# FFN-up with 512-column matmuls: rows and their remainders pass one rounded weight together, and ScalarE, VectorE and GpSimd share the rest

## The chip, the cores and the metric

The kernel runs on one core of a Trainium2 chip. The metric is the time of one execution on the device in microseconds (us), the median of several runs. The engines are called PE (TensorE), ACT (ScalarE), DVE (VectorE), POOL (GpSimd) and SP (SyncE, which issues most DMAs). The trace is of one profiled execution; its times are counted from the start of the span.

## The reference

The program computes two transformer blocks for 256 tokens of width 1024: first attention with a mixture of 32 experts, then a second block that ends with a gated feed-forward network (FFN). Only the FFN's first half is touched by the change:

```python
D_FF_2 = 2816
FFN_CONV_W = 3
...
        h = rms_norm(x, g_pre_ffn[l])
        up = causal_dwconv(h @ w_up[l].astype(h.dtype), w_conv_ffn[l], b_conv_ffn[l])
        c_u, c_g = jnp.split(up, 2, axis=-1)
        ffn = (jax.nn.gelu(c_g, approximate=True) * c_u) @ w_down[l].astype(h.dtype)
        x = x + rms_norm(ffn, g_post_ffn[l])
```

`w_up` is 1024 x 5632. The convolution runs over positions, three taps for each of the 5632 channels.

## The kernel before

**Rounded matmuls in three parts.** PE multiplies in a rounded fp32 format. To keep precision each operand is split in a rounded part (hi) and a remainder (lo), and a product is hi·hi + hi·lo + lo·hi. Each loaded megabyte of weights (128 x 2048 values) has a number s in the list `SPL` of splits; 34 to 55 are the 22 loads of `w_up`, 56 to 66 those of `w_down`. ACT rounds (`split`, L768) into one of two buffers of the tensor `W`, in turn, so the rounding of s waits until PE has done s-2. DVE then makes the remainder (`split`, L1237), and PE waits for that with `lo_done(s)`. The rows of h, turned so that the 256 tokens lie along the free dimension, are in `X`: `xin[0]` is X's rounded part, `xin[1]` its remainder, each with eight blocks k of 128 channels.

**FFN-up.** Split 34 + i' holds 256 output channels, taken as two banks of PSUM (m = 0, 1), each 128 channels x 256 tokens. The banks of the stage are `U_cv[0]` to `U_cv[43]`, n = 4i + 2·half + m, where i runs over 11 pairs of splits, half 0 is the branch u and half 1 the branch g. PE computes a bank in `columns_in`, by `mm3` (L1952): for each of eight k three matmuls of 256 columns, with the weight (hi, hi, lo) as stationary operand, so 48 for a split. `columns_first` (L2036) does split 34, part by part.

**After PE.** For each bank ACT makes `tmp` = last tap times bank plus bias (Identity, L1210); DVE adds the other two taps, shifted by one and two tokens, reading the bank in PSUM (L1920 and L1923), and the second of them releases the bank. When both banks of a g half are done, ACT takes GELU of them (L1215) and DVE multiplies the branches into `fT` (L1929). ACT and DVE work strictly in the order in which the program issues. In the loop over i, half, m, with m = 1, the rounding (ACT) and the remainder (DVE) of split 36 + 2i + half stand ahead of that bank's own work.

**The down projection.** For 22 blocks k of f, ACT rounds fT (`inner`, L1194) and DVE makes the remainder (L1904) into `X`, whose blocks come free as PE leaves them. The first six are issued inside the FFN-up loop, ahead of the last bank's work (i = 10, half = 1, m = 1). PE then runs 264 matmuls of 512 columns. Before any of them it waits for the remainder of split 56 and of block 0 of f.

GpSimd's part in the neighbourhood are three products in the recurrent layer before the FFN (L745 to L751) and four products with the gain of a norm (L728); it has nothing to do in the FFN. SP refills a slot of the ring of eight when DVE has made the remainder of the split that lay there.

## Time and profile before

| | us |
|---|---|
| median of 3 runs | 1410.02 (1408.59 to 1410.97) |
| profiled execution, span from first to last instruction | 1408.3 |
| PE busy (6969 matmuls) | 1286.9 (91%) |
| DVE busy | 486.8 (35%) |
| ACT busy | 401.2 (28%) |
| POOL busy | 59.1 (4%) |
| mean granted PE clock | 0.986 of full speed |

The profiled execution has no time of its own beside its span; the median lies 1.7 us above it. About two thirds of the span is the mixture of experts, bound by DMA; the FFN-up stage lies between 1212 and 1342 us, the down projection between 1342 and 1402. A row of the timeline reads: start, duration, engine, line and operation, output<-inputs, partitions x columns, count; in brackets the idle time of that engine before it and who ended that. Instructions on DVE and ACT overlap their neighbour by 0.05 to 0.1 us, so the distance from start to start is a little shorter than a duration. Durations of matmuls contain the way through the array; only their spacing tells what one costs. A row of the windows view gives the stretch, its length, then busy us and instructions of PE, PE's weight loads, DVE, ACT and POOL, then the granted PE clock as a share of full speed, the share of DMA and its GB/s. A row by line and form gives the count, then busy us, mean ns of one, idle before.

### The profile page before, as it was taken

To read this page: it belongs to the slowest core of one execution; us is meant where nothing else is said; L and a number is where in the kernel's file an instruction comes from. 1 tells how busy PE (TensorE), PEld (TensorE's weight loads), DVE (VectorE), ACT (ScalarE), POOL (GpSimd) and SP (SyncE) were. 2 spreads that over 40 slices of the span, in tenths; PEclk is the share of its full clock that TensorE was granted. 3 is DMA by queue.
4 is the path that set the end of the run, shared out by engine and by line. 5 is a ranking of instruction groups with operands and counts; after the bars stand their busy time and mean duration, and the time that the engine had idled before them with its cause. 6 is when DMAs were issued, how large, how long until landed. Compare 5 with 4: busy or idle time off the path is not lost.

```text
span 1408.3 us, 16583 instructions
## 1 busy us (share of the span) xinstructions
PE 1286.9 (91%) x6969; PEld 737.3 (52%) x6969; DVE 486.8 (35%) x730; ACT 401.2 (28%) x643; POOL 59.1 (4%) x115
## 2 busy tenths in 40 slices
PE   8999999999999889998888988889888999899998
PEld 7888433343333333333333332333324898799986
DVE  5895312112111111111211111111114687677765
ACT  5684212100110001100001000010004766655554
POOL 4001000000000000000000000000000510000000
PEclk9999899999999999999999999999999999899999
DMA  9548699999999999999999999999999964355520
GB/s 337 165 148 307 259 393 429 428 427 427 426 428 427 429 428 426 429 426 427 428 427 428 428 428 427 428 427 428 426 429 370 245 213 150 121 184 186 188 100 30
DMA packets 78474, 480.79 MB, mean 341 GB/s; under 512 B 5504, under 2 KB 40475, under 8 KB 53568
## 3 DMA queue, kind: packets, MB, share of 16 engines
q1 hardware_dynamic: 75904, 474.76, 83.3%
q0 software_dynamic: 2496, 4.96, 1.7%
q8 instruction: 57, 0.93, 0.3%
q14 instruction: 17, 0.14, 0.0%
HBM read 478.39 MB, written 1.31 MB: 341 GB/s over the span
## 4 chain that ended last, share of the span: by engine, by line
PE 52%; DMA 38%; DVE 4%; ACT 3%; issue 1%; DVEq 0%; ACTq 0%
DMA arena<-in_w_dn_dram 38%; PE ps L1952 22%; PE ps L2357 11%; PE ps L2397 11%; PE ps L2324 1%; PE ps L2413 1%; DVE W L1237 1%; PE ps L2036 1%; PE ps L1960 1%; PE ps L2514 1%; PE ps L2287 1%; ACT arena L960 0%; ACT arena L910 0%; PE ps L2368 0%; ACT W L768 0%
## 5 line engine op out<-in xcount | busy, mean ns | idle before, releaser
L2357 PE MATMUL ps<-ring,arena 128*64 128x512 f32 x1392 | 316.5, 597 | 12.0 <-DMA ring<-in_w_gu_dram 12.0
L2357 PEld LDWEIGHTS ps<-ring,arena 128*64 128x64 f32 x1392 | 97.4, 137 | 210.1 <-issue 179.1
L1952 PE MATMUL ps<-X,W 128*128 128x256 f32 x1560 | 191.4, 286 | 2.2 <-DVE W L1243 1.9
L1952 PEld LDWEIGHTS ps<-X,W 128*128 128x128 f32 x1560 | 190.2, 194 | 3.3 <-DVE W L1243 2.3
L1588 DVE TENSOR_SCALAR arena<-ps 128x512 f32<-128x512 f32 x32 | 22.1, 692 | 479.1 <-PE ps L2357 479.1
L1952 PE MATMUL ps<-W,X 128*128 128x512 f32 (+2 forms) x780 | 172.8, 380 | 2.7 <-issue 1.6
L1237 DVE TENSOR_TENSOR W<-ring,W 128x2048 fp32r<-128x2048 f32 (+2 forms) x64 | 144.9, 2264 | 78.9 <-ACT W L768 78.9
L2397 PE MATMUL ps<-ring,arena 128*64 128x512 f32 x648 | 145.7, 594 | 21.9 <-DMA ring<-in_w_dn_dram 21.9
L1952 PEld LDWEIGHTS ps<-W,X 128*128 128x128 f32 x780 | 141.5, 188 | 31.0 <-DVE W L1237 3.8
L973 ACT ACTIVATE arena<-arena 128x512 f32<-128x512 f32 x32 | 20.2, 630 | 460.2 <-DVE arena L1588 460.2
L2357 PE MATMUL ps<-arena 128*64 128x512 f32 x656 | 150.5, 599 | 0.0
L768 ACT ACTIVATE W<-ring 128x2048 fp32r<-128x2048 f32 (+2 forms) x65 | 122.6, 1887 | 81.5 <-PE ps L1952 80.5
L2397 PEld LDWEIGHTS ps<-ring,arena 128*64 128x64 f32 x648 | 48.4, 137 | 116.4 <-issue 115.8
L2397 PE MATMUL ps<-arena 128*64 128x512 f32 x376 | 85.8, 598 | 23.9 <-DMA arena<-in_w_dn_dram 23.9
L1616 DVE SCALAR_TENSOR_TENSOR X<-ps,arena,X 128x512 fp32r<-128x512 f32 x32 | 24.0, 751 | 219.7 <-ACT X L986 219.7
L986 ACT ACTIVATE X<-ps,arena 128x512 fp32r<-128x512 f32 x32 | 22.0, 687 | 258.4 <-PE ps L2397 258.4
L2357 PEld LDWEIGHTS ps<-arena 128*64 128x64 f32 x656 | 46.9, 138 | 91.1 <-issue 90.4
L2397 PEld LDWEIGHTS ps<-arena 128*64 128x64 f32 x376 | 25.1, 136 | 84.1 <-DMA arena<-in_w_dn_dram 42.4
L2324 PEld LDWEIGHTS ps<-X,W 128*128 128x128 f32 x256 | 33.7, 197 | 25.5 <-issue 24.9
L716 POOL CAST W<-arena 128x128 fp32r<-128x128 f32 x32 | 9.3, 293 | 871.0 <-PE ps L2357 851.4
L2413 PE MATMUL ps<-X,W 64*128 64x512 f32 x256 | 39.4, 425 | 6.5 <-DVE X L1616 6.5
L2368 PE MATMUL ps<-ident,arena 128*128 128x128 f32 x128 | 21.5, 291 | 25.6 <-ACT arena L960 25.6
(350 smaller groups left out, 991.4 us busy)
## 6 DMA issues: line engine op xcount, KB each, us to landing
ring<-in_w_gu_dram SPq DMA_DIRECT2D x87, 2048.0 KB, 22.4
ring<-in_w_dn_dram SPq DMA_DIRECT2D x40, 2048.0 KB, 24.5
arena<-in_w_gu_dram SPq DMA_DIRECT2D x39, 2048.0 KB, 20.4
arena<-in_w_dn_dram SPq DMA_DIRECT2D x23, 2048.0 KB, 25.6
ring<-in_w_up_dram SPq DMA_DIRECT2D x22, 1024.0 KB, 5.1
ring<-in_w_in_dram SPq DMA_DIRECT2D x15, 1024.0 KB, 12.6
ring<-in_w_down_dram SPq DMA_DIRECT2D x11, 1024.0 KB, 4.9
ring<-in_w_o_dram SPq DMA_DIRECT2D x4, 1024.0 KB, 4.9
```

The lines of the kernel that those rows point to most:

```text
L768: e.activation(halved(s)[0], loads[n][0], ACT.Copy).then_inc(s_hi, 1)
L973: e.activation(sig, glu, ACT.Sigmoid, scale=1.702).then_inc(s_sig, 1)
L986: e.activation(yhi[x % 2], ps[:, DB, :], ACT.Copy, scale=gs[:, x:x + 1]).then_inc(s_yhi, 1)
L1237: e.tensor_tensor(lo, loads[SPL[s]][0], hi.bitcast(F32), ALU.subtract).then_inc(s_lo, 1)
L1588: e.tensor_scalar(glu, whole(gb), 7.0, None, ALU.min).then_inc(s_glu, 1)
L1616: e.scalar_tensor_tensor(out=ylo[x % 2], in0=ps[:, DB, :], scalar=gs[:, x:x + 1], in1=yhi[x % 2].bitcast(F32), op0=ALU.mult, op1=ALU.subtr ...
L1952: y = e.matmul(o, l, r, start=start and i == 0, stop=stop and i == 2)
L2324: y = e.matmul(ps[:, x[0], a * 256:(a + 1) * 256], part[:, t, k * P:(k + 1) * P], Sr[j % 2][:, t], start=part is uhi and t == 0, stop=part ...
L2357: y = e.matmul(ps[c * 64:c * 64 + 64, use[0], :], xs[:, k, c0:c0 + CAP], w[:, half * D + c * 512:half * D + (c + 1) * 512], start=False, s ...
L2368: y = e.transpose(ps[:, TB, j * P:(j + 1) * P], actv[:, j * P:(j + 1) * P], ident[:, :])
L2397: y = e.matmul(ps[c * 64:c * 64 + 64, DB, :], a, w[:, c * 512:(c + 1) * 512], start=kk == 0, stop=kk == KD - 1)
L2413: y = e.matmul(ps[:, b, :], GTr[x // 2 % 2][q, x % 2, t * P:(t + 1) * P], part[x % 2][q, :], start=x == 0 and part is yhi, stop=x == NE - ...
```

## The change

Four things change in FFN-up; all else stays.

1. For splits 35 to 55 PE runs `wide_columns`: for each k one matmul of 512 columns with the rounded weight, whose moving operand is X's rounded rows and their remainders (two pieces of 256), into both halves of the bank, and one of 256 columns with the weight's remainder into the first half. Split 34 (`wide_first`) keeps three parts of 256, the third into the second half.
2. A bank's two halves must be added. ACT copies the second half to an SBUF buffer `zs` (eight of them, `second_half(n)`), issued one bank ahead. DVE adds the first half to it (`summed(n)`), also one bank ahead, and that add releases the bank. Identity and both convolution steps then read `zs`. Identity waits for the release.
3. GpSimd multiplies the branches into `fT`.
4. DVE makes seven eighths of a remainder (splits 36 to 55), GpSimd block 7 of it; PE waits for that before k = 7 of m = 0, and SP before it refills the slot.

```diff
@@ sync
                     e.wait_ge(*unloaded(b))
+                    if 36 <= order.get(b, 0) < 56:
+                        e.wait_ge(s_lo_end, order[b] - 35)
@@ gpsimd
+            for i in range(11):
+                for half in range(2):
+                    s = 36 + 2 * i + half
+                    if s < 56:
+                        hi, lo = halved(s)
+                        e.wait_ge(s_hi, s + 1)
+                        e.tensor_tensor(lo[:, 7:8], loads[SPL[s]][0][:, 7:8], hi[:, 7:8].bitcast(F32),
+                                        ALU.subtract).then_inc(s_lo_end, 1)
+                for m in range(2):
+                    y = 4 * (i % 2) + m
+                    e.wait_ge(s_cv, 4 * i + m + 1)
+                    e.wait_ge(s_ggelu, 2 * i + m + 1)
+                    e.tensor_tensor(fT[:, 2 * i + m, :], tmp[y], tmp[y + 2], ALU.mult).then_inc(s_f, 1)
@@ scalar
+            def second_half(n):
+                x = U_cv[n]
+                e.wait_ge(*BK.filled(x))
+                if n >= 8:
+                    e.wait_ge(s_cv, n - 7)
+                e.activation(zs[n % 8], ps[:, x[0], T:2 * T], ACT.Copy).then_inc(s_half2, 1)
...
                         if m:
                             split(36 + 2 * i + half)
+                        if 4 * i + 2 * half + m < 43:
+                            second_half(4 * i + 2 * half + m + 1)
                         if i >= 2:
                             e.wait_ge(s_f, 2 * (i - 2) + m + 1)
-                        e.wait_ge(*BK.filled(x))
-                        e.activation(tmp[y], ps[:, x[0], 0:T], ACT.Identity, scale=col("w_conv_ffn_2b", c),
+                        e.wait_ge(*BK.emptied(U_cv[4 * i + 2 * half + m]))
+                        e.activation(tmp[y], zs[(4 * i + 2 * half + m) % 8], ACT.Identity, scale=col("w_conv_ffn_2b", c),
...
-                    e.wait_ge(*BK.emptied(U_cv[4 * i + 2 + m]))
+                    e.wait_ge(s_cv, 4 * i + 3 + m)
                     e.activation(tmp[y + 2], tmp[y + 2], ACT.Gelu_apprx_tanh).then_inc(s_ggelu, 1)
@@ vector
+            def summed(n):
+                x = U_cv[n]
+                e.wait_ge(s_half2, n + 1)
+                e.tensor_tensor(zs[n % 8], ps[:, x[0], 0:T], zs[n % 8], ALU.add).then_inc(taken[x[0]], 1)
...
-                        if m:
+                        if m and i < 10:
+                            split(36 + 2 * i + half, 7)
+                        elif m:
                             split(36 + 2 * i + half)
+                        if n < 43:
+                            summed(n + 1)
                         e.wait_ge(s_conv, n + 1)
-                        step(e.scalar_tensor_tensor(out=y[:, 1:], in0=ps[:, x[0], 0:T - 1], scalar=col("w_conv_ffn_2", 44 + c),
+                        step(e.scalar_tensor_tensor(out=y[:, 1:], in0=z[:, 0:T - 1], scalar=col("w_conv_ffn_2", 44 + c),
...
-                        e.scalar_tensor_tensor(out=y[:, 2:], in0=ps[:, x[0], 0:T - 2], scalar=col("w_conv_ffn_2", c),
-                                               in1=y[:, 2:], op0=ALU.mult, op1=ALU.add).then_inc(taken[x[0]], 1)
-                for m in range(2):
-                    y = 4 * (i % 2) + m
-                    e.wait_ge(*BK.emptied(U_cv[4 * i + m]))
-                    e.wait_ge(s_ggelu, 2 * i + m + 1)
-                    e.tensor_tensor(fT[:, 2 * i + m, :], tmp[y], tmp[y + 2], ALU.mult).then_inc(s_f, 1)
+                        e.scalar_tensor_tensor(out=y[:, 2:], in0=z[:, 0:T - 2], scalar=col("w_conv_ffn_2", c),
+                                               in1=y[:, 2:], op0=ALU.mult, op1=ALU.add).then_inc(s_cv, 1)
@@ tensor
+            def wide_columns(s, m, use, ks):
+
+                hi, lo = halved(s)
+                c, o = slice(m * P, (m + 1) * P), ps[:, use[0], :].rearrange("p (a t) -> p a t", a=2)
+                for k in ks:
+                    if k == 7 and m == 0 and s >= 36:
+                        e.wait_ge(s_lo_end, s - 35)
+                    if k < KD - 1:
+                        e.matmul(o, hi[:, k, c], X[:, :, k, :], start=k == 0, stop=False)
+                        y = e.matmul(o[:, 0], lo[:, k, c], xin[0][:, k, :], start=False, stop=False)
+                    else:
+                        e.matmul(o[:, 0], lo[:, k, c], xin[0][:, k, :], start=False, stop=False)
+                        y = e.matmul(o, hi[:, k, c], X[:, :, k, :], start=False, stop=True)
+                return y
```

DVE in the middle of the stage, before, one pair of splits. L1237 is a remainder, L1920 and L1923 the two convolution steps of a bank, L1929 the product of the branches:

```order
L1237 TENSOR_TENSOR W<-ring,W 128x2048
L1920 SCALAR_TENSOR_TENSOR arena<-ps,cols,arena 128x255
L1923 SCALAR_TENSOR_TENSOR arena<-ps,cols,arena 128x254
L1920 SCALAR_TENSOR_TENSOR arena<-ps,cols,arena 128x255
L1923 SCALAR_TENSOR_TENSOR arena<-ps,cols,arena 128x254
L1237 TENSOR_TENSOR W<-ring,W 128x2048
L1920 SCALAR_TENSOR_TENSOR arena<-ps,cols,arena 128x255
L1923 SCALAR_TENSOR_TENSOR arena<-ps,cols,arena 128x254
L1929 TENSOR_TENSOR arena<-arena 128x256 x2
```

DVE at the same place, changed. L1265 is the remainder, L1938 the add of the next bank's halves, L1959 and L1962 the two steps:

```order
L1265 TENSOR_TENSOR W<-ring,W 128x1792
L1938 TENSOR_TENSOR arena<-ps,arena 128x256
L1959 SCALAR_TENSOR_TENSOR arena<-arena,cols 128x255
L1962 SCALAR_TENSOR_TENSOR arena<-arena,cols 128x254
L1938 TENSOR_TENSOR arena<-ps,arena 128x256
L1959 SCALAR_TENSOR_TENSOR arena<-arena,cols 128x255
L1962 SCALAR_TENSOR_TENSOR arena<-arena,cols 128x254
L1265 TENSOR_TENSOR W<-ring,W 128x1792
```

The add of a bank stands behind the remainder of a split and ahead of the steps of the bank before; the product has left the queue.

ACT at the same place, before: L1210 is Identity, L768 the rounding of a split, L1215 GELU:

```order
L1210 ACTIVATE arena<-ps,cols 128x256
L768 ACTIVATE W<-ring 128x2048
L1210 ACTIVATE arena<-ps,cols 128x256 x2
L768 ACTIVATE W<-ring 128x2048
L1210 ACTIVATE arena<-ps,cols 128x256
L1215 ACTIVATE arena<-arena 128x256 x2
```

ACT there, changed: L1209 is the copy of the second half, L1238 Identity, L786 the rounding, L1243 GELU:

```order
L1209 ACTIVATE arena<-ps 128x256
L1238 ACTIVATE arena<-arena,cols 128x256
L786 ACTIVATE W<-ring 128x2048
L1209 ACTIVATE arena<-ps 128x256
L1238 ACTIVATE arena<-arena,cols 128x256
L1209 ACTIVATE arena<-ps 128x256
L1238 ACTIVATE arena<-arena,cols 128x256
L786 ACTIVATE W<-ring 128x2048
L1209 ACTIVATE arena<-ps 128x256
L1238 ACTIVATE arena<-arena,cols 128x256
L1243 ACTIVATE arena<-arena 128x256 x2
```

Each rounding now has a copy and an Identity ahead of it that read the work of other engines. At the end of the stage the copy of the last bank (the last L1209) and an Identity stand ahead of the six roundings of f (L1221):

```order
L1209 ACTIVATE arena<-ps 128x256
L1238 ACTIVATE arena<-arena,cols 128x256
L1221 ACTIVATE X<-arena 128x256 x6
L786 ACTIVATE W<-ring 128x2048
L1238 ACTIVATE arena<-arena,cols 128x256
L1243 ACTIVATE arena<-arena 128x256 x2
```

Before, only the two L1210 that fall between the roundings of splits 56 and 57 stood there.

## Rows read from the trace of the kernel before

**Rows 1.** Windows view: busy time by engine in one stretch of FFN-up.
```profile
1246.00:1266.00 20.00, 20.00 (x169) 20.00 (x168) 15.80 (x20) 9.99 (x13) 0.00 (x0) 1.00 0.53 171
```

**Rows 2.** Timeline, FFN-up: ACT's roundings that wait for PE, two splits apart.
```profile
1249.60 1.91 ACT L768 ACTIVATE W<-ring 128x2048 fp32r<-128x2048 f32 x1 [2.25 <-PE ps L1952]
...
1261.12 1.91 ACT L768 ACTIVATE W<-ring 128x2048 fp32r<-128x2048 f32 x1 [2.25 <-PE ps L1952]
```

**Rows 3.** Timeline, down projection: ACT's roundings, one split of 24 matmuls apart.
```profile
1353.86 1.92 ACT L768 ACTIVATE W<-ring 128x2048 fp32r<-128x2048 f32 x1 [2.91 <-PE ps L1952]
...
1359.30 1.92 ACT L768 ACTIVATE W<-ring 128x2048 fp32r<-128x2048 f32 x1 [2.91 <-PE ps L1952]
```

**Rows 4.** Timeline, FFN-up, ACT and DVE: from a convolution's end to the next.
```profile
1242.75 0.48 DVE L1923 SCALAR_TENSOR_TENSOR arena<-ps,cols,arena 128x254 f32<-128x254 f32 x1
...
1243.26 0.42 ACT L1215 ACTIVATE arena<-arena 128x256 f32<-128x256 f32 x1 [2.51 <-DVE arena L1923]
1243.59 0.55 ACT L1210 ACTIVATE arena<-ps,cols 128x256 f32<-128x256 f32 x1
...
1244.04 1.90 ACT L768 ACTIVATE W<-ring 128x2048 fp32r<-128x2048 f32 x1
...
1245.97 2.29 DVE L1237 TENSOR_TENSOR W<-ring,W 128x2048 fp32r<-128x2048 f32 x1 [0.80 <-ACT W L768]
...
1248.18 0.47 DVE L1920 SCALAR_TENSOR_TENSOR arena<-ps,cols,arena 128x255 f32<-128x255 f32 x1
1248.69 0.48 DVE L1923 SCALAR_TENSOR_TENSOR arena<-ps,cols,arena 128x254 f32<-128x254 f32 x1
```

**Rows 5.** Groups by line and form, whole span, nearest to the new operations.
```profile
L1237 DVE TENSOR_TENSOR W<-ring,W 128x2048 fp32r<-128x2048 f32 x60 | 137.9, 2299 | 77.0 <-ACT W L768 77.0
...
L1243 DVE TENSOR_TENSOR W<-ring,W 128x1024 fp32r<-128x1024 f32 x2 | 2.4, 1222 | 0.0
...
L1762 DVE SCALAR_TENSOR_TENSOR arena<-arena,cols 128x255 f32<-128x255 f32 x4 | 1.9, 484 | 0.1
...
L1752 DVE TENSOR_TENSOR arena<-ps,arena 128x256 f32<-128x256 f32 x2 | 0.8, 419 | 0.0
...
L960 ACT ACTIVATE arena<-ps,gp 128x256 f32<-128x256 f32 x64 | 26.8, 470 | 41.6 <-PE ps L2324 41.6
...
L968 ACT ACTIVATE arena<-ps 128x512 f32<-128x512 f32 x32 | 19.1, 597 | 27.5 <-PE ps L2368 27.5
```

**Rows 6.** Timeline near 1106: DVE and POOL products together; POOL's at 1024 columns.
```profile
1105.54 0.69 DVE L1711 TENSOR_TENSOR arena<-arena 128x512 f32<-128x512 f32 x1
1105.54 1.84 POOL L728 TENSOR_TENSOR arena<-h,arena 128x512 f32<-128x512 f32 x1 [2.93 <-DVE h L1713]
1106.26 1.67 DVE L1713 TENSOR_TENSOR h<-h,arena 128x512 f32<-128x512 f32 x1
...
1108.01 1.27 POOL L728 TENSOR_TENSOR arena<-h,arena 128x512 f32<-128x512 f32 x1 [0.63 <-DVE h L1713]
...
1147.43 2.37 POOL L745 TENSOR_TENSOR arena<-arena 128x1024 f32<-128x1024 f32 x1 [28.71 <-ACT arena L1105]
```

**Rows 7.** Timeline at the seam from FFN-up to the down projection.
```profile
1339.40 2.12 ACT L1194 ACTIVATE X<-arena 128x256 fp32r<-128x256 f32 x6
...
1341.76 1.92 ACT L768 ACTIVATE W<-ring 128x2048 fp32r<-128x2048 f32 x1 [0.24 <-PE ps L1952]
...
1342.68 9.56 PE L1952 MATMUL ps<-W,X 128*128 128x512 f32 x41 [0.96 <-issue]
```

**Rows 8.** Timeline of PE after two gaps, then the windows view there.
```profile
1076.56 1.21 PE L2413 MATMUL ps<-X,W 64*128 64x512 f32 x8 [1.57 <-DVE X L1616]
1078.48 3.41 PE L1960 MATMUL ps<-ident,h 128*128 128x128 f32 x16 [0.71 <-DVE h L1697]
...
1076.00:1080.00 4.00, 2.73 (x15) 2.26 (x16) 3.18 (x4) 3.00 (x5) 0.84 (x1) 0.76 1.06 390
1080.00:1084.00 4.00, 4.00 (x20) 3.62 (x20) 3.95 (x9) 3.97 (x9) 0.00 (x0) 0.81 1.06 368
```

More of the change, by code:

```diff
@@ L246, in build_program @@
         tmp = [ar(5632 + 256 * i, T) for i in range(8)]
+        zs = [ar(12288 + 256 * i, T) for i in range(8)]
         rows, used = {}, [0, 0, 0, 0]
@@ L1232, in step, with split @@
                 x.then_inc(own.sem, own.up())
-            def split(s):
+            def split(s, nk=None):
                 hi, lo = halved(s)
                 e.wait_ge(s_hi, s + 1)
-                e.tensor_tensor(lo, loads[SPL[s]][0], hi.bitcast(F32), ALU.subtract).then_inc(s_lo, 1)
+                e.tensor_tensor(lo[:, 0:nk], loads[SPL[s]][0][:, 0:nk], hi[:, 0:nk].bitcast(F32), ALU.subtract).then_inc(s_lo, 1)
             def first_split(half):
```

36 lines of the change are left out of this document (30 added, 6 removed).

## Prediction

> **What bounds the kernel now.** I read the busy table by slices first: TensorE (PE) is at 0.9 or more nearly everywhere. The windows of the FFN-up stage, which is where the change works, show PE busy for all of its time at granted clock 1.00 (the 2.4 GHz level), VectorE (DVE) for 0.79 of it, ScalarE (ACT) for about half, GpSimd (POOL) never [rows 1]. Then the timeline of two engines gives the price of one matmul. ACT's rounding of split s waits for the last bank of split s-2, so its starts beat at PE's pace: 1249.60 and 1261.12 enclose two splits, 96 matmuls of 256 columns, 11.52 us, or 120.0 ns each [rows 2]. In the down projection the same roundings are 5.44 us apart for 24 matmuls of 512 columns, 226.7 ns each [rows 3]. At 2.4 GHz 256 columns stream in 106.7 and 512 in 213.3 ns: every matmul costs its columns plus 13.3 ns. That 13.3 is all that wide matmuls can save.
>
> Last, who has slack behind PE. For each pair of splits (four banks) ACT waits 2.51 us for VectorE's convolution before a GELU and 2.25 us for PE before a rounding [rows 2, 4]. The remainder that PE needs next is done at 1245.97+2.29 = 1248.26, and PE begins with it when it has finished the split before, near 1249.5. So ACT, DVE and PE lie about 1.2 us apart. This margin decides the case.
>
> **PE's part.** Splits 35 to 55 (21 of the 22) go from 48 to 32 matmuls each: 16 x (226.7 + 120.0) ns = 5.55 us instead of 5.76. A pair takes 11.09 instead of 11.52 us, and the stage saves 336 x 13.3 ns = **4.5 us**, if nobody else comes late. Split 34 keeps its 48 matmuls. No row shows a moving operand in two pieces of 256; between 226.7 and twice 120.0 ns I take 226.7, the columns and one fixed part.
>
> **What ACT, VectorE and GpSimd get, per pair.** ACT gets four copies of 256 from PSUM: 597 ns for 512 columns less 256 at ACT's rate gives 0.39, 470 ns with a gain [rows 5] is the upper end; I take 0.40, 0.30 from start to start. Its Identity now reads SBUF; I keep 0.55. VectorE gets four adds of 256 (0.42 by the row of a product from PSUM and SBUF; I take 0.41) and loses two products and an eighth of each remainder: 2.30 us at 2048 and 1.22 at 1024 columns make 1.05 ns a column, so 1792 cost 2.02 and 1.94 from start to start. Its convolution steps now read two SBUF operands; such a step takes 484 ns, as now [rows 5]. The totals are harmless: ACT about 7.9, VectorE 9.0 of 11.09 us. GpSimd gets four products of 256: 1.27 us at 512 and 2.37 at 1024 columns [rows 6] give 0.72 each, 2.9 us a pair. SP now waits for GpSimd's eighths too before it refills a slot, but the ring holds eight loads and none is needed within a pair.
>
> **The new wait is what costs.** So far ACT's Identity of a bank waited only for PE. Now it waits until VectorE has added the bank's halves, and that add stands in VectorE's queue behind the remainder. So the next rounding can't begin until the last remainder is done: rounding and remainder, which overlapped across two engines, become one chain. From start to start, from one GELU to the same GELU a pair later, by the steps of [rows 4] (GELU to next 0.33, Identity to rounding 0.45, rounding to remainder 1.93, first convolution step to second 0.51, that one to GELU 0.51):
> GELU 0.33, copy 0.30, Identity 0.45, rounding 1.93, remainder 1.94, add and release 0.44, Identity 0.45, rounding 1.93, remainder 1.94, add 0.33, two convolution steps 1.02. The sum is **11.06 us**, just PE's new 11.09. Before, the second Identity and rounding hung on PE alone, and this loop had over 2 us to spare.
>
> **The lock.** VectorE and GpSimd hold each other up in this trace. At 1105.54 both start a product of two SBUF operands, released by the same instruction. VectorE's takes its 0.69 us; GpSimd's takes 1.84 instead of 1.27, as if begun when the other ended. VectorE's next, at 1106.26, takes 1.67: it ends 0.55 after GpSimd's [rows 6]. An instruction so held ends its own time less 0.13 after the other's end. Now GpSimd's eighth and VectorE's remainder are released together by the rounding. The remainder goes first (0.03 us after ACT's end in [rows 4], GpSimd 0.08 after its releaser in [rows 6]); the eighth then holds the interface for 0.59 after it. The add (PSUM and SBUF) I take as free; the first convolution step ends 0.21 later. GpSimd's branch product, queued behind the eighth, comes between the two steps and delays the second by 0.43. The loop is 11.06 + 0.64 = **11.7 us**, above the old 11.52.
>
> Here the Trainium skill speaks against the change: "SBUF — State Buffer", section "Who interferes with whom", says that any VectorE instruction with two SBUF inputs contends with a GpSimd instruction that reads SBUF, exclusively, whoever comes first. The rows show it for products of two tensors only; for the fused convolution step no row does. By the page the result is the forecast's 1414.1, by the letter of the rows 1408.6.
>
> **The sum.** Up to bank 7 PE runs at its own pace: three wide splits save 0.21 each, -0.6 us. The first turn of the loop brings +0.4 (11.94 by the same steps), the eight pairs after it 0.19 each, +1.5. The last bank of the stage comes **+1.3 us** against before.
>
> Then the seam to the down projection. Now PE resumes at 1342.68, 0.9 us after the last bank was full at 1341.76 [rows 7]; ACT had rounded the first six blocks of f in the meantime. In the new order a copy of the last bank stands before these roundings, and on VectorE the remainder of split 56 ends 0.6 us after the last bank. Behind it stand add, two steps, add, two steps, then the first remainder of f: from its next start at +0.54, 0.33 + 0.51 + 0.40 + 0.33 + 0.51 + 0.40 is +3.0, and 0.52 more until PE starts: 3.5 instead of 0.9, **+2.6 us**. A further 0.2 comes when split 58 is late. In all +4.1: span 1408.3 + 4.1 = 1412.4. The median of the runs is 1.7 above the span, which gives **1414.1 us**. With the doubtful durations at their ends (GpSimd 0.62 to 0.80, copy 0.38 to 0.43, Identity 0.52 to 0.58) the same walk gives +2.3 to +5.8: 1412.3 to 1415.8.
>
> **Rivals.** (1) The lock doesn't catch the convolution steps. The loop is 11.06, PE's 11.09 binds but for 0.2 every other pair, the last bank comes 3.45 us earlier, and the seam costs 2.0: -1.45, **1408.6**. For it: no row shows such a step held. Against: it reads two SBUF operands like the product that was held.
> (2) Faster: the loop fits and the seam is found hidden, or Identity from SBUF takes 0.45. All of PE's 4.5 us gives **1405.5**, with a seam of 2 us 1407.5. Against: the seam's steps follow from queue order alone, without the lock.
> (3) GpSimd goes first: its eighth takes the interface before the remainder. Both remainders lie on the loop, each 0.59 later; the loop is about 12.4, 0.7 more in each of nine pairs: **1420**. It decides from the point where GpSimd starts within 0.03 us of ACT's end; [rows 6] speak for VectorE.
> (4) The clock falls at the seam. PE stands idle for 3.7 us there. After a gap of 1.57 us and one of 0.71 the granted clock fell to 0.5 for 3.4 us in all (0.24 and 0.19 of two stretches of 4 us, over 0.5) [rows 8]. In a dense stretch half of that is lost, +1.7: **1415.8**, up to 1417. Against: the 0.96 us of now had no such end.
>
> **The numbers.** Forecast 0.47 (0.38 of it above 1412.8), rival 1 0.18, rival 2 0.12, rival 3 0.10, rival 4 0.13. A measurement of this kernel can tell about 0.2%, 2.8 us: faster means below 1407.2 (rival 2: 0.12), slower above 1412.8 (0.38 + 0.10 + 0.13 = 0.61), the rest is 0.27. The range 1407.4 to 1418.5 leaves out rival 2's lower part and rival 3, about 0.2.
>
> **What would show it.** In the profile after: matmuls of 512 and 256 in turn, 0.35 us a pair of them. PE idle about 0.6 us once in four banks, waiting for a VectorE remainder. ACT's Identity waiting for VectorE's add, not for PE. GpSimd's eighths at about 2.6 us instead of 0.72, and convolution steps well above 0.48 in the mean. A gap of 3.5 us or so before the first 512-column matmul of the down projection. If the steps stay at 0.48, rival 1 holds; if remainders take 2.6, rival 3; if the spacing of the wide matmul is 240, PE's part was never there. I am wrong too if copy and Identity are much cheaper from SBUF, since twelve steps in a row carry any error of one.

## The result, and the profile after

The changed kernel takes **1415.36 us** (median of 6 runs, 1412.85 to 1417.89) against 1410.12 us for the kernel before (6 runs beside it, 1408.39 to 1410.97). The ratio is 1.0038, 95% interval 1.0028 to 1.0048: slower by 5.2 us. The forecast was 1414.1 in a range of 1407.4 to 1418.5. The profiled execution has a span of 1413.9 us and a time of its own of 1415.59; the one of before had a span of 1408.3.

The two traces agree up to the first matmul of FFN-up (1212.09 us before, 1212.12 after). The last VectorE instruction ends 5.6 us later, so the whole loss lies between. It falls into three parts:

| from, to | before | after | difference |
|---|---|---|---|
| first matmul of FFN-up to last bank full | 129.67 | 131.28 | +1.61 |
| last bank full to the first down-projection matmul | 0.92 | 3.28 | +2.36 |
| that matmul to the start of the last VectorE group | 61.66 | 63.25 | +1.59 |

The busy totals of the page of after. GpSimd now has 157 instructions, it had 115; PE has 6633, it had 6969, and is as busy as it was:

```profile
PE 1285.8 (91%) x6633; PEld 717.8 (51%) x6633; DVE 497.4 (35%) x752; ACT 415.7 (29%) x687; POOL 129.0 (9%) x157
```

The groups by line and shape over 1220 to 1345 us of after (line, engine, operation, output<-input, count | busy us, mean ns | idle before and who ended it). The first two lines are GpSimd's two new tasks, then VectorE's remainder of 1792 columns, ACT's Identity, the two convolution steps and the new add:

```profile
L763 POOL TENSOR_TENSOR W<-ring,W 128x256 fp32r<-128x256 f32 x20 | 51.5, 2575 | 98.6 <-ACT W L786 98.6
...
L769 POOL TENSOR_TENSOR arena<-arena 128x256 f32<-128x256 f32 x20 | 16.6, 829 | 8.7 <-ACT arena L1243 8.7
...
L1265 DVE TENSOR_TENSOR W<-ring,W 128x1792 fp32r<-128x1792 f32 x20 | 40.5, 2026 | 10.8 <-ACT W L786 10.8
L1238 ACT ACTIVATE arena<-arena,cols 128x256 f32<-128x256 f32 x43 | 25.6, 595 | 1.8 <-DVE arena L1938 1.1
L1962 DVE SCALAR_TENSOR_TENSOR arena<-arena,cols 128x254 f32<-128x254 f32 x42 | 23.9, 569 | 1.5
L1959 DVE SCALAR_TENSOR_TENSOR arena<-arena,cols 128x255 f32<-128x255 f32 x42 | 23.1, 550 | 0.8
L1938 DVE TENSOR_TENSOR arena<-ps,arena 128x256 f32<-128x256 f32 x44 | 18.5, 420 | 11.2 <-ACT arena L1209 11.2
```

The steps stood at 484 ns before [rows 5]; now 550 and 569. An eighth of a remainder keeps GpSimd busy for 2575 ns, since it stands still while VectorE takes the other seven eighths. The waits of the same stretch (who waited for what: total, times, longest):

```profile
PEld ps L2645 <- DVE W L1265: 4.8, 9, 0.7
...
ACT arena L1238 <- DVE arena L1938: 1.1, 4, 0.4
```

PE, which after its first matmul waited for nobody in this stage before, now waits nine times for a remainder of VectorE. Why it is late is read from one turn of the timeline (start, us, engine, line, operation, idle before). Two splits, four banks, lie between the first and the last of these rows:

```profile
1262.32 1.90 ACT L786 ACTIVATE W<-ring 128x2048 fp32r<-128x2048 f32 x1
...
1264.25 2.02 DVE L1265 TENSOR_TENSOR W<-ring,W 128x1792 fp32r<-128x1792 f32 x1 [0.23 <-ACT W L786]
1264.30 2.58 POOL L763 TENSOR_TENSOR W<-ring,W 128x256 fp32r<-128x256 f32 x1 [2.33 <-ACT W L786]
...
1266.19 0.42 DVE L1938 TENSOR_TENSOR arena<-ps,arena 128x256 f32<-128x256 f32 x1
1266.53 0.63 DVE L1959 SCALAR_TENSOR_TENSOR arena<-arena,cols 128x255 f32<-128x255 f32 x1
1266.83 0.92 POOL L769 TENSOR_TENSOR arena<-arena 128x256 f32<-128x256 f32 x1
1267.19 0.84 DVE L1962 SCALAR_TENSOR_TENSOR arena<-arena,cols 128x254 f32<-128x254 f32 x1
1268.07 0.42 ACT L1243 ACTIVATE arena<-arena 128x256 f32<-128x256 f32 x1 [2.32 <-DVE arena L1962]
1268.39 0.36 ACT L1209 ACTIVATE arena<-ps 128x256 f32<-128x256 f32 x1
...
1268.66 0.59 ACT L1238 ACTIVATE arena<-arena,cols 128x256 f32<-128x256 f32 x1
...
1269.15 1.90 ACT L786 ACTIVATE W<-ring 128x2048 fp32r<-128x2048 f32 x1
...
1271.08 2.02 DVE L1265 TENSOR_TENSOR W<-ring,W 128x1792 fp32r<-128x1792 f32 x1 [0.80 <-ACT W L786]
...
1273.02 0.38 ACT L1209 ACTIVATE arena<-ps 128x256 f32<-128x256 f32 x1 [1.22 <-PE ps L2649]
1273.03 0.42 DVE L1938 TENSOR_TENSOR arena<-ps,arena 128x256 f32<-128x256 f32 x1
...
1273.54 0.60 ACT L1238 ACTIVATE arena<-arena,cols 128x256 f32<-128x256 f32 x1
1274.05 1.90 ACT L786 ACTIVATE W<-ring 128x2048 fp32r<-128x2048 f32 x1
```

Leave out GpSimd's two rows and the copy of 1273.02, and each row starts when the one before it ends or releases it: rounding, remainder, add, two steps, GELU, copy, Identity, rounding, remainder, add, Identity, and the next rounding. The copy of 1273.02 waits for PE and isn't what holds the Identity of 1273.54: a copy and the Identity behind it start 0.27 us apart (1268.39, 1268.66), here 0.52. It closes on itself after 1274.05 - 1262.32 = **11.73 us**, and over 1262.32 to 1332.70 the mean of six turns is 11.73 too. In the kernel before a pair took 11.52 [rows 2], at PE's pace. At 1266.53 the first convolution step, beside the tail of the eighth, takes 0.63; at 1267.19 the second, beside the branch product, 0.84.

The seam, in the timeline, answers to [rows 7]:

```profile
1343.40 0.38 ACT L1209 ACTIVATE arena<-ps 128x256 f32<-128x256 f32 x1 [1.22 <-PE ps L2649]
1343.67 0.42 DVE L1938 TENSOR_TENSOR arena<-ps,arena 128x256 f32<-128x256 f32 x1
...
1344.92 0.42 DVE L1938 TENSOR_TENSOR arena<-ps,arena 128x256 f32<-128x256 f32 x1
...
1345.76 0.48 DVE L1962 SCALAR_TENSOR_TENSOR arena<-arena,cols 128x254 f32<-128x254 f32 x1
1346.16 2.10 DVE L1932 TENSOR_TENSOR X<-arena,X 128x256 fp32r<-128x256 f32 x6
...
1346.68 1.65 PE L1986 MATMUL ps<-W,X 128*128 128x512 f32 x5 [3.31 <-issue]
```

The last bank is full at 1343.40 and PE resumes at 1346.68. The wait is named "issue", but VectorE's rows tell what it is: the remainders of the f blocks stand behind two adds and four steps. And the clock, in windows (busy time by engine, then the granted clock):

```profile
1344.00:1348.00 4.00, 1.32 (x5) 1.15 (x6) 3.93 (x12) 3.81 (x8) 0.00 (x0) 0.96 0.68 259
1348.00:1352.00 4.00, 4.00 (x12) 3.09 (x12) 3.77 (x4) 1.23 (x3) 1.97 (x1) 0.62 0.20 18
1352.00:1356.00 4.00, 4.00 (x19) 3.33 (x18) 1.34 (x4) 3.02 (x5) 0.74 (x1) 1.00 0.63 249
```

After the gap PE runs at the 1.2 GHz level for part of two windows: 0.04 x 4 + 0.38 x 4 = 1.7 us of full clock are missing, 12 matmuls of 512 columns where the next window has 19.

### The profile page after: what moved, and what is told of

The parts are those of the page before. It is cut to its first block, busy times and chain, and to the rows that moved or that the text cites. A ratio compares the mean times of both kernels' runs of the same rounds, so it can differ in the third digit from the quotient of the medians.

```text
span 1413.9 us, 16075 instructions
## 1 busy us (share of the span) xinstructions
PE 1285.8 (91%) x6633; PEld 717.8 (51%) x6633; DVE 497.4 (35%) x752; ACT 415.7 (29%) x687; POOL 129.0 (9%) x157
## 4 chain that ended last, share of the span: by engine, by line
PE 44%; DMA 39%; DVE 9%; ACT 6%; issue 2%; ACTq 0%; DVEq 0%; SPq 0%
DMA arena<-in_w_dn_dram 38%; PE ps L1986 14%; PE ps L2391 11%; PE ps L2431 11%; DVE W L1265 4%; ACT W L786 3%; PE ps L2358 1%; PE ps L2447 1%; PE ps L2670 1%; DVE arena L1962 1%; PE ps L1994 1%; PE ps L2548 1%; PE ps L2321 0%; ACT arena L978 0%; ACT arena L928 0%
## 5 line engine op out<-in xcount | busy, mean ns | idle before, releaser
L1265 DVE TENSOR_TENSOR W<-ring,W 128x2048 fp32r<-128x2048 f32 (+3 forms) x64 | 139.6, 2181 | 66.9 <-ACT W L786 66.9
L786 ACT ACTIVATE W<-ring 128x2048 fp32r<-128x2048 f32 (+2 forms) x65 | 122.5, 1884 | 59.1 <-PE ps L1986 58.4
L2645 PE MATMUL ps<-X,W 128*128 128x512 f32 x294 | 106.3, 401 | 1.9 <-DVE W L1265 1.9
L2646 PE MATMUL ps<-X,W 128*128 128x256 f32 x294 | 82.5, 281 | 0.0
L1986 PE MATMUL ps<-X,W 128*128 128x256 f32 x552 | 69.7, 289 | 2.2 <-DVE W L1271 1.9
L1986 PEld LDWEIGHTS ps<-X,W 128*128 128x128 f32 x552 | 68.6, 197 | 3.3 <-DVE W L1271 2.3
L2645 PEld LDWEIGHTS ps<-X,W 128*128 128x128 f32 x294 | 55.3, 188 | 16.3 <-DVE W L1265 4.8
```

Source lines behind the costliest of these rows:

```text
L786: e.activation(halved(s)[0], loads[n][0], ACT.Copy).then_inc(s_hi, 1)
L1265: e.tensor_tensor(lo[:, 0:nk], loads[SPL[s]][0][:, 0:nk], hi[:, 0:nk].bitcast(F32), ALU.subtract).then_inc(s_lo, 1)
L1986: y = e.matmul(o, l, r, start=start and i == 0, stop=stop and i == 2)
L2645: e.matmul(o, hi[:, k, c], X[:, :, k, :], start=k == 0, stop=False)
L2646: y = e.matmul(o[:, 0], lo[:, k, c], xin[0][:, k, :], start=False, stop=False)
```

## Experiments

Medians carry some noise from ahead of the stage: its first matmul starts anywhere from 1210.5 to 1213.3 us in these traces. So beside each median stands the stage's own length in the profiled execution, from its first matmul to the end of the last VectorE group ("FFN"). That length has noise of its own. In every one of these traces the stage begins at a granted clock of 0.50, which rises to 1.00 at differing moments (5.9 us after the first matmul before, 4.4 in e1). So split 34, which is the same work in all kernels but for where its third part goes, takes anything from 7.82 to 8.51 us ("split 34", from the stage's first matmul to that of split 35), and two FFN lengths can differ by 0.7 us for that alone. Also shown: the time of two splits ("pair"), PE's idle time at the seam, and the time from PE's resumption to the start of the last VectorE group ("rest"). All but the medians and ratios are read from one execution of each kernel.

| kernel | split 34 | pair | idle at the seam | clock falls there | rest | FFN | median us | ratio to before |
|---|---|---|---|---|---|---|---|---|
| before | 8.51 | 11.52 | 0.96 | no | 61.66 | 193.66 | 1410.12 | |
| after | 8.45 | 11.73 | 3.31 | yes | 63.25 | 199.22 | 1415.36 | 1.0038 |
| e1_pe_alone | 7.82 | 11.28 | 1.21 | no | 61.65 | 190.67 | 1407.84 | 0.9981 |
| e2_gp_writes | 8.47 | 11.34 | 2.93 | no | 61.66 | 193.62 | 1411.02 | 1.0013 |
| e3_all_ve | 7.99 | 11.75 | 3.11 | yes | 63.26 | 198.67 | 1415.25 | 1.0037 |
| e4_warm | 8.03 | 11.73 | 0.67 | no | 61.68 | 197.22 | 1414.30 | 1.0026 |
| e5_pipe | 8.48 | 11.28 | none | no | | 191.50 | 1407.24 | 0.9986 |
| e6_pipe_ve | 7.95 | 11.28 | none | no | | 189.80 | 1406.24 | 0.9974 |
| e7_product_back | 8.04 | 11.42 | 3.02 | yes | 63.24 | 195.69 | 1412.76 | 1.0021 |
| e8_eighth_back | 8.09 | 11.90 | 3.26 | yes | 64.46 | 201.50 | 1417.68 | 1.0055 |
| e9_seam | 8.09 | 11.73 | 2.07 | no | 62.52 | 196.85 | 1413.27 | 1.0023 |
| e10_grouped | 8.45 | 11.17 | none | no | | 189.27 | 1405.99 | 0.9974 |

The kernel before ran beside each set: 1409.87 us (e1 to e4), 1409.28 (e5, e6, e7, e9) and 1409.94 (e8, e10).

### The wide matmuls alone

The kernel before with TensorE's part of the change and nothing else.

```diff
-                    columns_in(34 + i, m, whole(x, T)).then_inc(full[x[0]], 1)
+                    wide_columns(34 + i, m, x, range(KD)).then_inc(full[x[0]], 1)
```

> The kernel before with PE's part alone: for splits 35 to 55 the 512-column matmul and the 256-column one, everything behind PE as before. The bank's second half (rounded weight times the remainders of the rows) is computed and never read, so that product is left out of the result. Theory (PE costs columns plus 13.3 ns per matmul, and the loss of the change lies wholly behind PE): bank pace 11.09 us a pair, stage 4.5 us shorter, the gap at the seam as before, time 4.5 us below before, 1405.6. Rival (a moving operand in two pieces streams no faster than two matmuls, 240 ns): a pair stays at 11.52 us and the time is that of before, 1410.

Measured: 1407.84 us, ratio 0.9981 (0.9972 to 0.9990); the pair is 11.28 us. So the wide operand does pay, but about half of what 13.3 ns for each matmul saved would give; the expected 11.09 and 1405.6 were missed. The timeline of e1 gives the price of the mix, 512 and 256 columns in turn:

```profile
1262.35 0.40 PE L2609 MATMUL ps<-X,W 128*128 128x512 f32 x1
1262.59 0.28 PE L2610 MATMUL ps<-X,W 128*128 128x256 f32 x1
1262.71 0.40 PE L2609 MATMUL ps<-X,W 128*128 128x512 f32 x1
```

Starts are 0.24, 0.12 us apart, 11.28 / 32 = 352.5 ns for the two, where [rows 2, 3] add up to 346.7. The ten pairs save 2.4 us. That the FFN is 3.0 us shorter is 0.7 split 34's doing.

### GpSimd that only writes

The change, with GpSimd's eighth and product replaced by fills of a constant, so the eighth and f are not computed; all waits stay. The fill of the eighth's place gets one wait more, for GpSimd's own last one.

```diff
-                        e.tensor_tensor(lo[:, 7:8], loads[SPL[s]][0][:, 7:8], hi[:, 7:8].bitcast(F32),
-                                        ALU.subtract).then_inc(s_lo_end, 1)
+                        if s > 36:
+                            e.wait_ge(s_lo_end, s - 36)
+                        e.memset(ar(14336, 2 * T), 0.5).then_inc(s_lo_end, 1)
...
-                    e.tensor_tensor(fT[:, 2 * i + m, :], tmp[y], tmp[y + 2], ALU.mult).then_inc(s_f, 1)
+                    e.memset(fT[:, 2 * i + m, :], 0.5).then_inc(s_f, 1)
```

> The changed kernel with every wait in place, but GpSimd only writes constants and reads nothing: 512 columns into an unused place instead of its eighth of a remainder (which is left as an older split's), 256 columns into fT instead of the product of the branches; both computations are left out. Theory (the exclusive interface adds 0.64 us a pair to a loop of 11.1): convolution steps back at 0.48 us, remainders 2.02, a pair at 11.1 to 11.2 us, last bank 5 us earlier than in the changed kernel, the gap at the seam still about 3.1 us with the low clock behind it; 4.5 to 6 us below the changed kernel, about 1410. Rival (GpSimd's queue is late by itself, without any interface): the waits for GpSimd stay, and the time stays at 1415. Rival (the chain of waits alone makes the loss): a pair stays at 11.7 and the time at 1415.

Measured: 1411.02 us, 1.0013 (1.0003 to 1.0023). The steps are back (groups by line and shape, 1220 to 1335 us):

```profile
L1963 DVE SCALAR_TENSOR_TENSOR arena<-arena,cols 128x254 f32<-128x254 f32 x41 | 19.8, 483 | 1.5
L1960 DVE SCALAR_TENSOR_TENSOR arena<-arena,cols 128x255 f32<-128x255 f32 x41 | 19.6, 478 | 0.8
...
L765 POOL MEMSET arena<- 128x512 f32 x20 | 10.6, 528 | 124.0 <-ACT W L787 124.0
```

The pair falls from 11.73 to 11.34, close to PE's 11.28, though not to the expected 11.1 to 11.2. The timeline tells how:

```profile
1261.42 2.02 DVE L1266 TENSOR_TENSOR W<-ring,W 128x1792 fp32r<-128x1792 f32 x1 [0.47 <-ACT W L787]
1261.44 0.53 POOL L765 MEMSET arena<- 128x512 f32 x1 [4.45 <-ACT W L787]
```

The fill runs beside the remainder, holds it for nothing (2.02 us) and doesn't have to wait for it, as the reading eighth did (2.58). So it is over long before the first step, and the branch product's fill, 0.31 us, is over before the next one too: between 1220 and 1335 us no fill runs beside a step. This run shows that the steps are back at 0.48 when GpSimd's reading instructions are gone; it doesn't show a step beside a fill. In this execution the seam of 2.93 us didn't bring the clock down.

### Both tasks back on VectorE

The change with whole remainders and the branch products on VectorE; GpSimd's two loops and the waits for them are gone.

```diff
-                        if m and i < 10:
-                            split(36 + 2 * i + half, 7)
-                        elif m:
+                        if m:
                             split(36 + 2 * i + half)
...
+                for m in range(2):
+                    y = 4 * (i % 2) + m
+                    e.wait_ge(s_cv, 4 * i + m + 1)
+                    e.wait_ge(s_ggelu, 2 * i + m + 1)
+                    e.tensor_tensor(fT[:, 2 * i + m, :], tmp[y], tmp[y + 2], ALU.mult).then_inc(s_f, 1)
```

> The changed kernel with GpSimd's two tasks given back to VectorE (whole remainders of 2048 columns, branch products in its own queue after a pair), so nothing can contend. Theory (chain of ACT and VectorE): the loop is 11.1 + 2 x 0.27 for the longer remainders = 11.7 us a pair, PE waits about 0.5 us a pair, the gap at the seam 3.4 us with low clock; 1413 to 1415.5, little different from the changed kernel. Rival (contention is the whole loss): with GpSimd gone the kernel is as fast as PE allows, 1406 to 1408.

Measured: 1415.25 us, 1.0037 (1.0023 to 1.0050); pair 11.75, steps 0.48. The lock is gone and nothing is won. Two remainders of 2048 columns instead of 1792 put 2 x 0.265 = 0.53 us on the loop, two steps without a hold take 0.15 + 0.36 = 0.51 off. In this order of the queues GpSimd's help is worth what its presence costs. With neither, by these numbers, the loop would be 11.22 us, below PE's 11.28.

e2, which has neither, took 11.34, and e7 below, with one hold of 0.15, took 11.42 and not 11.37. Their timelines show a link that the sum leaves out: the new copy of the next bank, which waits for PE and stands in ACT's queue ahead of the Identity. In e2 the add ends at 1270.10, the copy starts at 1270.07, released by PE, and the Identity at 1270.35, so there the copy sets it. When the loop gets short, PE's banks come into it that way.

### The two tasks apart

The product alone back on VectorE, and the eighth alone (each is half of the edit above).

> The change, but the branch product is VectorE's again; GpSimd keeps only the last eighth of the remainders. With both tasks on VectorE the pair took 11.75 us, with both on GpSimd 11.73. Theory A (the eighth shortens the loop by two remainders, 2 x 0.27 us, and the product gives 0.5 of it back by holding the second step): pair 11.75 - 0.53 + 0.15 for the first step beside the eighth = 11.37 us; steps 0.50 and 0.48; seam as in the change (3.1 to 3.3 us). FFN start to end 199.2 - 10 x 0.36 = 195.6 us, 1.7 less still if the clock doesn't fall; median 1410.5 to 1412. Rival B (the product doesn't lie on the loop): pair stays at 11.7, FFN 199 us, median 1415.

> The change, but the remainders are VectorE's again in full; GpSimd keeps only the branch product. The four corners so far: both on VectorE, pair 11.75 us; eighth alone on GpSimd, 11.42; both on GpSimd, 11.73. Theory A (the product on GpSimd only costs the loop, by holding the second step from 0.48 to 0.84 once and 0.63 once in four banks, while its 0.42 us on VectorE did not lie in the loop): pair 11.75 + 0.15 to 0.3 = 11.9 to 12.05 us, FFN start to end 198.7 + 1.5 to 3 = 200 to 202 us, the clock falling at the seam, median 1416 to 1418.5. Rival B (the product's 0.42 us per pair of banks was in the loop on VectorE, so that GpSimd frees as much as it costs): pair 11.6 to 11.8, median 1414.5 to 1415.5.

Measured: product back, 1412.76 us, 1.0021 (1.0012 to 1.0030), pair 11.42. Eighth back, 1417.68 us, 1.0055 (1.0042 to 1.0069), pair 11.90. Theory A holds in both, and nearly in size: FFN 195.69 where 195.6 was expected, 201.5 where 200 to 202 was. The first is a little luck, since split 34 took 0.4 us less than in the changed kernel and the pair 0.05 more than expected; the second has 1.2 us in it from a clock that stayed low for longer. For e7 the median lies 0.8 above 1412, the end of its range with the clock falling in the gap, as it did. In e8 GpSimd's product now starts early and catches the first step instead of the second (timeline, VectorE and GpSimd):

```profile
1266.42 1.26 POOL L761 TENSOR_TENSOR arena<-arena 128x256 f32<-128x256 f32 x1 [8.51 <-ACT arena L1235]
...
1267.34 0.62 DVE L1949 SCALAR_TENSOR_TENSOR arena<-arena,cols 128x255 f32<-128x255 f32 x1
```

It was released while the remainder ran (1264.80 to 1267.09), took 1.26 instead of 0.74 and held the step for 0.15: 11.75 + 0.15 = 11.90. The product's 0.42 us on VectorE never lay on the loop; moving it could only cost. The eighth's did, and is the only useful half of what GpSimd took.

### The gap filled

The change with 12 matmuls of 512 columns of no use put between the last bank and the down projection, to keep PE busy; results are untouched.

```diff
+                if k == 0 and t == 0:
+                    claim(U_dd[0][0])
+                    e.wait_ge(s_hi, s + 1)
+                    for j in range(12):
+                        e.matmul(whole(U_dd[0][0]), hi[:, 0, 0:P], hi[:, 0, 0:512], start=True, stop=True)
```

> The changed kernel with twelve idle matmuls of 512 columns (2.7 us) on PE in the gap between FFN-up and the down projection, on operands that are ready, into a bank that the first real matmul then overwrites. Theory (the gap lets the granted clock fall to 1.2 GHz for 3.4 us of dense work, which costs 1.7 us): no stretch at the low clock behind the seam, 1.7 us below the changed kernel, 1413.7. Rival (the fall costs nothing or comes from elsewhere): time as the changed kernel, 1415.4.

Measured: 1414.30 us, 1.0026 (1.0016 to 1.0037). The rest of the stage takes 61.68 us, as before, instead of 63.25, with the clock at 1.00. First PE's timeline at the seam, then the windows:

```profile
1343.64 2.89 PE L2700 MATMUL ps<-W 128*128 128x512 f32 x12
1347.19 1.16 PE L1986 MATMUL ps<-W,X 128*128 128x512 f32 x4 [0.67 <-DVE X L1932]
```

```profile
1344.00:1348.00 4.00, 3.33 (x16) 2.45 (x15) 3.93 (x12) 3.57 (x9) 0.00 (x0) 1.00 0.60 214
1348.00:1352.00 4.00, 4.00 (x19) 3.31 (x18) 3.79 (x5) 1.70 (x3) 1.98 (x1) 1.00 0.12 48
```

So the third part of the loss is the clock, 1.6 us of it, and in this trace it comes back when PE doesn't stand idle. The median alone couldn't tell: it is 1.1 us below the changed kernel's, 0.6 above the expected 1413.7, and the two ratios' intervals overlap.

### The seam in another order

The change, with the first six f blocks ahead of the last bank's copy and add, in ACT's queue and in VectorE's (one of the two edits):

```diff
-                        if m and i == 10 and half:
-                            for k in range(6):
-                                inner(k)
...
+                        if i == 10 and half and not m:
+                            for k in range(6):
+                                inner(k)
                         if n < 43:
                             summed(n + 1)
```

> The change with one edit: the first six f blocks (rounding on ACT, remainder on VectorE) stand ahead of bank 43's copy and add in both queues, and not behind them. Theory A: pair unchanged at 11.73 us; at the seam VectorE goes from the remainder of 1343.7 to the add of bank 42, two steps and then the f remainders, so TensorE resumes about 2.0 us after the last bank is full and not 3.3: 1.3 us less, and up to 1.7 us more if the clock then doesn't fall. FFN start to end 199.2 becomes 196.2 to 197.9; median 1412.4 to 1414.1. Rival B (the gap is set by the last bank's own work, not the order): 3.3 us as before, median 1415.

Measured: 1413.27 us, 1.0023 (1.0013 to 1.0034), pair 11.73, gap 2.07, no fall of the clock. FFN is 196.85, within the 196.2 to 197.9 expected. Of the 1.6 us that the clock gave back 0.9 were lost again: the rest takes 62.52 and not 61.65. The timeline has the wait for it. After 48 matmuls PE stands still until 1357.90, released by the remainder of split 58 (1355.55 to 1357.84), about 0.8 us later than 48 times 226.7 ns behind 1346.23. That split's rounding stands in ACT's queue behind a GELU, which waited 3.18 us for the last bank's convolution steps, and these stand behind the remainder of split 57, the first of them held to 0.96 us beside GpSimd's product. In e4 the same remainder starts at 1355.53, in time for a PE that resumed 0.96 us later. So the last bank's chain set the end of it in e9, once the first gap was shorter.

### ACT's and VectorE's queues in another order

The change, with each split's place in the two queues shifted: VectorE takes the add of the odd bank, the remainder, the next add, and only then the steps; on ACT both Identities stand behind the rounding. GELU and the branch products (with GpSimd's queue) move back with them by one split, and the first six blocks of f stand ahead of the last banks' steps. So these two runs test the loop and the seam together.

```diff
+            for j in range(22):
+                summed(2 * j + 1)
+                split(36 + j, 7 if j < 20 else None)
+                if j < 21:
+                    summed(2 * j + 2)
+                if j >= 20:
+                    for k in range(2) if j == 20 else range(2, 6):
+                        inner(k)
+                taps(2 * j)
+                taps(2 * j + 1)
```

> The change, with the queues of ACT and VectorE written in another order: of each two banks, ACT copies the odd bank's second half, then rounds, then the two Identities, then copies the next bank's half; VectorE adds the odd bank, takes the remainder, adds the next bank and only then takes the steps; the first f blocks stand ahead of the last banks' work. Same arithmetic, same engines. Theory A (the time was lost because the Identity waits for an add that stands behind a remainder, in a closed loop of 11.73 us per pair, and because the f blocks stand behind the last bank at the seam): the pair falls from 11.73 to what TensorE needs, 11.28 us as in the kernel with the wide stream alone; TensorE waits for no remainder; the first product of the down projection starts about 0.1 to 0.9 us after the last bank is full and not 3.3; the clock stays at 1.00 there. FFN start to end 199.2 becomes 190.7 to 191.8 us, the median 1407 to 1409. Rival B (GpSimd's presence is the cost, by the lock or because it comes late with its eighth): the steps stay at 0.55 us and the pair stays above 11.6; median 1412 or more.

> As the kernel with the new order, but VectorE takes the remainders whole and the branch products itself; GpSimd does nothing in the stage. Theory A: with the closed loop gone TensorE is the bound with or without GpSimd, pair 11.28 us, VectorE has 20 x 0.27 and 44 x 0.2 us more work beside TensorE but no lock; the seam is the same or 0.3 us shorter; the median is within 1 us of that kernel's, 1406 to 1409, and below the kernel before. Rival B (GpSimd's help is what makes the new order reach TensorE's pace): the pair is above 11.45 us and TensorE waits for remainders again.

Measured: 1407.24 us, 0.9986 (0.9977 to 0.9996) with GpSimd, 1406.24, 0.9974 (0.9964 to 0.9983) without. Both run at 11.28 us a pair. In e5 the steps are held more than ever, at no cost to the pair (groups, 1220 to 1335 us; then the waits of 1220 to 1350):

```profile
L1965 DVE SCALAR_TENSOR_TENSOR arena<-arena,cols 128x255 f32<-128x255 f32 x40 | 26.4, 661 | 0.0
L1968 DVE SCALAR_TENSOR_TENSOR arena<-arena,cols 128x254 f32<-128x254 f32 x40 | 22.6, 564 | 1.4
```

```profile
ACT arena L1216 <- PE ps L2673: 39.5, 21, 2.2
```

ACT again waits for PE, up to 2.2 us, and PE for no remainder. So neither the work nor the lock was too much for 11.28 us: the order of the queues made a loop of them. GpSimd costs e5 something only at the end: its FFN is 1.7 us longer than e6's, 0.5 of that by split 34. Its last products come late, the f remainders wait for them, and with them the remainder of a down-projection split:

```profile
1346.50 1.68 POOL L769 TENSOR_TENSOR arena<-arena 128x256 f32<-128x256 f32 x2 [7.61 <-ACT arena L1243]
1346.62 1.84 DVE L1950 TENSOR_TENSOR X<-arena,X 128x256 fp32r<-128x256 f32 x2
...
1348.39 2.28 DVE L1283 TENSOR_TENSOR W<-ring,W 128x2048 fp32r<-128x2048 f32 x1
...
1350.72 1.65 PE L2010 MATMUL ps<-W,X 128*128 128x512 f32 x6 [1.01 <-DVE W L1283]
```

### Matmuls of one size together

e6 with the matmuls of a bank grouped by size: seven of 512, eight of 256, one of 512.

```diff
+                if len(ks) == KD:
+                    for k in range(KD - 1):
+                        e.matmul(o, hi[:, k, c], X[:, :, k, :], start=k == 0, stop=False)
+                    for k in range(KD):
+                        e.matmul(o[:, 0], lo[:, k, c], xin[0][:, k, :], start=False, stop=False)
+                    return e.matmul(o, hi[:, KD - 1, c], X[:, :, KD - 1, :], start=False, stop=True)
```

> The new queue order with both tasks on VectorE (1406.2 us, pair 11.28, TensorE without a wait), with one edit on TensorE: in each bank the seven first matmuls of 512 columns stand together, then the eight of 256, then the last of 512, where they alternated one by one; the last bank keeps its order. A 512 in a stream of its own takes 226.7 ns, a 256 takes 120.0, the sum is 346.7, but alternating they took 352.5 ns. Theory A (a change of size from one matmul to the next costs about 3 ns each): 13 of 15 changes in a bank fall away, pair 11.28 to 11.11 us, 10 pairs 1.7 us less, median 1404.5 to 1405. Rival B (the 5.8 ns belong to the wide operand's two-part access, or the narrow one's, in whatever order): pair stays at 11.28, median 1406.2.

Measured: pair 11.17 us, between the two. A bank had 14 changes of size and has two (not 13 fewer of 15, as expected beforehand), so with 12 fewer in each of four banks a change costs 0.11 / 48 = 2.3 ns, against the 3 of theory A. One bank of the timeline reads 1276 to 1279 as

```profile
1275.77 1.53 PE L2649 MATMUL ps<-X,W 128*128 128x512 f32 x6
1277.15 1.12 PE L2651 MATMUL ps<-X,W 128*128 128x256 f32 x8
1278.10 0.40 PE L2652 MATMUL ps<-X,W 128*128 128x512 f32 x1
```

eight matmuls of 256 in 0.95 us, 119 ns each. The median, 1405.99 us, 0.9974 (0.9963 to 0.9985), can't be told from that of e6, and the expected 1404.5 to 1405 was missed. The FFN of the profiled executions is 0.5 us shorter though split 34 took 0.5 longer, so from split 35 on it is 1.0 shorter, about the 1.1 of ten pairs. Of the 5.8 ns more per couple, grouping takes off 3.4. The other 2.4 stay open; the two changes left in a bank would make 0.6 of them.

## Why the prediction was right, and where it wasn't

**PE's part.** Mis-sized. The term was 336 x 13.3 ns = 4.5 us, a pair 11.09; a pair takes 11.28 at PE's pace (e1, e5, e6), and the 21 splits save 336 x 7.5 ns = 2.5 us. The step that failed is adding the prices of two pure streams for a mixed one. It cost the forecast little, because PE didn't set the pace, but it made the rivals that end faster look nearer than they were: of "all of PE's 4.5 us, 1405.5" only 1407.8 was there.

**The loop.** Right. It was put at 11.7 us by 12 steps and measured at 11.73; each of its links stands in the turn shown above. Two errors in it cancel. Without the lock it was put at 11.06 and is 11.22 (11.75 - 0.53 by e3, 11.73 - 0.51 by the turn): Identity from SBUF takes 595 ns and not 550, so that Identity to rounding is 0.49 and 0.51, not 0.45, and from add to Identity it is 0.51, not 0.44. The lock was put at 0.64 and is 0.51. The check on this is e6 and e5: what the loop's explanation says must vanish with the order does vanish, in both to 11.28. What the walk left out is that the new copy ties the Identity to PE as well; it costs nothing at 11.73, but 0.05 us a pair in e7, and e2 stays 0.06 above PE's pace. That is read from the timelines; no run tests it.

**The lock.** Its mechanism was right: the remainder goes first, the eighth is caught for its whole length (2575 ns; "about 2.6"), the add from PSUM is free (420 ns), both fused steps are held. Sizes: first step +0.15 where +0.21 was put, second +0.36 where +0.43 was. Rival 1 (the steps aren't caught) and rival 3 (GpSimd goes first) are out: 550 and 569 ns instead of 484, and remainders at 2026. The rule of the Trainium skill, "SBUF — State Buffer", section "Who interferes with whom", holds here for the fused step, 0.63 and 0.84 us beside a GpSimd instruction that reads, 0.48 where none does (e2, e3).

What the prediction didn't ask is whether GpSimd's help is worth its lock. The four corners are 11.75 (neither on GpSimd, e3), 11.42 (the eighth alone, e7), 11.90 (the product alone, e8) and 11.73 (both). The eighth gains 0.53 a pair and costs 0.20 alone and 0.36 beside the product; the product gains nothing and costs 0.15 alone and 0.31 beside the eighth, behind which it comes late and catches the second step.

**Last bank.** +1.3 forecast, +1.61 measured. The forecast's form was right: splits 35 to 37 pass at PE's own pace, and the rest is nine turns. Nine times 0.21 above the old pair and 0.2 more in the first turn make 2.1; the three splits give back 0.4 and not 0.6, since they save 0.12 and not 0.21 each.

**The seam.** PE was to resume 3.5 us after the last bank, and did after 3.28; +2.6 forecast, +2.36 measured. The walk from the first add to the first remainder of f was right (2.49 measured, 2.48 put); VectorE's remainder of split 56 was over 0.35 us after the last bank and not 0.6, so the walk began 0.27 earlier. Its cause, the f remainders behind the last banks' adds and steps, is tested by e9 (2.07) and e5, e6 (no gap).

**The clock.** Rival 4, with a chance of 0.13, is what happened, on top of the main forecast: it put the price at +1.7 for a total of 1415.8, and the stage's rest is 1.59 us longer, the profiled run's time 1415.59. The row that made me rate it low was the 0.96 us gap of now, which is no row for a gap of 3.7. The rows at hand for longer gaps [rows 8] did show a fall. The median of 1415.36 is between the forecast and the rival. The forecast's 1414.1 was short by 1.3, and the clock accounts for it: 1.6 + 2.4 + 1.6 = 5.6 against a sum of 4.1 (with 0.2 for split 58 in it, which I found no sign of in this trace). So the nearness of the number is part luck. The clock's 1.6 and 0.3 of the last bank were missing, 0.2 of the seam and 0.2 for split 58 were too much; and the median lies 0.4 from rival 4 and 1.3 from the forecast.

Of what was said to show it, PE's idle time (0.45 us a pair, put at 0.6), the spacing of 0.35 us, the eighths, the steps and the gap all came as told. The only sign that came weaker is Identity waiting for the add: 4 times and 1.1 us in the waits view, since in most turns the copy ahead of it waits for PE until shortly before the add ends, so that hardly any idle time is left to put down to the add. It is no less a link of the loop: the Identity starts 0.51 after the add's start.

## What to carry to other kernels

Before an edit that lets one engine wait for another in a new place, write down the chain from each instruction back to itself one iteration later, across the queues; if it comes near the pace of the bound engine, the order of the queues decides, and it can be mended there (e5 and e6: the same work, 7 to 9 us faster than after, by the ratios and by the medians). A helper engine pays only where its piece lies on that loop, and pays less where it reads the same memory as the engine that it relieves. At a seam between stages, put what the next stage's first instruction needs ahead of the leftovers of the last one; a gap costs its length, and in the four traces here with 3.0 to 3.3 us of idle time the clock's fall as well.

## What the hardware showed that I had not expected

Matmuls of 512 and 256 columns in turn take 352.5 ns a couple, while each size in its own stream takes 226.7 and 120.0. Grouped by size within a bank they take 349 (11.17 / 32), which makes a change of size about 2 ns here.

The fall of the clock after the seam, one execution of each kernel. Idle times of 0.67, 0.96, 1.21, 2.07 and 2.93 us there had no fall behind them; 3.02, 3.11, 3.26 and 3.31 did, and cost 1.6 us in three cases. In e8, after 3.26, it lasted longer, at 0.50 in windows of one microsecond up to 1354, and cost 2.8. [Rows 8] show a fall after shorter gaps in another stretch, so the length of one gap is not the whole condition; what more there is stays open.

A constant fill by GpSimd (528 ns for 512 columns) beside VectorE's remainder of two SBUF operands holds neither: the remainder takes its 2.02 us, and the fill doesn't wait. The eighth of a remainder, which reads, does wait there (2.58 us) and holds the first step behind for 0.15; a branch product holds the second for 0.36, and in e5 and e9 a step beside one takes 0.96 us instead of 0.48.
